# A decoder block with 32 experts on one core: order of the first value products, of the first experts' residues, and of six embedding products

## What is computed

```
h = rmsnorm(x, mix_norm);  proj = h @ w_in
ya = hgrn2_mix(...);  yb = retention_mix(...)
merged = sigmoid(ga) * (ya @ w_branch_a) + sigmoid(gb) * (yb @ w_branch_b)
x = x + merged @ w_out
h2 = rmsnorm(x, ffn_norm)
x = x + hier_moe(h2, ...)      # y_e = (silu(x_e @ w_gate) * (x_e @ w_up)) @ w_down, weighted sum of 2 experts
hp = rmsnorm(x, ple_norm)
x = x + sigmoid(hp @ w_ple_gate) * (p @ w_ple_proj)
return rmsnorm(x, final_norm)
```

## Time and profile before

| | us |
|---|---|
| timed executions | 1492.79, 1492.96, 1490.2 |
| median | 1492.79 |
| the profiled execution | 1489.6 |
| its span, first to last instruction | 1487.8 |
| PE busy | 1431.0 |
| DVE busy | 765.4 |
| ACT busy | 597.1 |
| GpSimd busy | 77.2 |

### The profile page before, as it was taken

One profiled execution on the slowest core, in us unless ns is written; L12 is line 12 of the kernel. 1 busy time (PEld: TensorE's weight loads), 2 busy tenths in 40 slices (PEclk: granted clock), 3 DMA queues, 4 the chain that ended last, 5 costly groups with the idle time before them and its releaser, 6 DMA issues.

```text
span 1487.8 us, 19084 instructions
## 1 busy us (share of the span) xinstructions
PE 1431.0 (96%) x7882; PEld 1192.9 (80%) x7882; DVE 765.4 (51%) x963; ACT 597.1 (40%) x731; POOL 77.2 (5%) x71
## 2 busy tenths in 40 slices
PE   6999999999999999999999999997899999998998
PEld 5888778877887888788888889986788888876886
DVE  5520266655553444221221125246799999987654
ACT  4410222212323322211111113243688888887555
POOL 0000000000000000000000000002122222211000
PEclk9999999999999999999999999998899999998999
DMA  6200111016220111221122218313899999995231
GB/s 242 85 2 0 49 30 30 15 32 154 57 57 8 50 54 39 67 68 56 60 63 63 63 50 299 133 71 129 348 372 384 391 381 393 384 369 214 85 107 64
DMA packets 103807, 205.26 MB, mean 138 GB/s; under 512 B 12976, under 2 KB 73008, under 8 KB 90160
## 3 DMA queue, kind: packets, MB, share of 16 engines
q1 hardware_dynamic: 93184, 182.89, 34.9%
q0 software_dynamic: 9248, 16.80, 3.0%
q10 hardware_dynamic: 1296, 4.46, 0.7%
HBM read 187.86 MB, written 28.84 MB: 146 GB/s over the span
## 4 chain that ended last, share of the span: by engine, by line
PE 52%; DVE 2%; DMA 1%; ACT 1%; issue 1%; POOLq 0%; DVEq 0%; ACTq 0%; SPq 0%
PE two_banks L176 8%; PE two_banks L178 8%; PE two_banks L177 8%; PE two_banks L2528 4%; PE two_banks L2529 4%; PE two_banks L2530 4%; PE two_banks L2411 2%; PE two_banks L2657 2%; PE two_banks L2413 2%; PE two_banks L2412 2%; PE two_banks L2658 2%; PE two_banks L2659 2%; PE two_banks L2518 2%; PE two_banks L2447 1%; DVE two_m_lo L1530 0%
## 5 line engine op out<-in xcount | busy, mean ns | idle before, releaser
L1332 DVE TENSOR_TENSOR two_chunk_lo<-two_chunk_raw,two_hi 128x2048 fp32r<-128x2048 f32 x96 | 217.2, 2286 | 21.8 <-ACT two_hi L1328 20.8
L1328 ACT CAST two_hi<-two_chunk_raw 128x2048 fp32r<-128x2048 f32 x96 | 180.9, 1917 | 7.3 <-DMA two_chunk_raw<-w_e 6.8
L223 DVE TENSOR_TENSOR mix_w_lo<-mix_w_raw,mix_w_hi 128x1024 fp32r<-128x1024 f32 (+1 forms) x51 | 58.5, 1148 | 194.0 <-ACT mix_w_hi L219 194.0
L176 PE MATMUL front_sums<-mix_hT_hi,mix_w_hi 128*128 128x512 f32 x320 | 127.7, 399 | 2.0 <-ACT reten_raw L892 2.0
L178 PE MATMUL front_sums<-mix_hT_hi,mix_w_lo 128*128 128x512 f32 x320 | 124.9, 390 | 0.0
L177 PE MATMUL front_sums<-mix_hT_lo,mix_w_hi 128*128 128x512 f32 x320 | 124.6, 389 | 0.0
L2528 PE MATMUL two_banks<-two_hi,two_xT_hi 128*128 128x512 f32 x256 | 104.0, 406 | 2.5 <-DVE two_xT_lo L1716 1.9
L219 ACT CAST mix_w_hi<-mix_w_raw 128x1024 fp32r<-128x1024 f32 (+1 forms) x51 | 50.4, 988 | 138.4 <-PE two_banks L178 88.2
L2530 PE MATMUL two_banks<-two_hi,two_xT_lo 128*128 128x512 f32 x256 | 101.5, 396 | 0.0
L2529 PE MATMUL two_banks<-two_chunk_lo,two_xT_hi 128*128 128x512 f32 x256 | 101.4, 396 | 0.0
L176 PE MATMUL two_banks<-mix_hT_hi,mix_w_hi 128*128 128x512 f32 x224 | 87.1, 389 | 0.0
(11 more groups left out here) (316 smaller groups left out, 3026.0 us busy)
## 6 DMA issues: line engine op xcount, KB each, us to landing
two_chunk_raw<-w_e SPq DMA_DIRECT2D x102, 1024.0 KB
mix_w_raw<-w_in SPq DMA_DIRECT2D x44, 512.0 KB, 3.9
two_r<-results SPq DMA_DIRECT2D x16, 512.0 KB, 4.9
vals_w_raw<-w_in SPq DMA_DIRECT2D x12, 512.0 KB, 8.2
heads_values<-x SPq DMA_DIRECT2D x8, 512.0 KB, 10.4
reten_swapped<-reten_raw SPq DMA_DIRECT2D x8, 512.0 KB, 6.3
mix_w_raw<-w_b SPq DMA_DIRECT2D x8, 512.0 KB, 4.6
two_x<-x SPq DMA_DIRECT2D x8, 512.0 KB, 7.4
```

What stands on the lines that cost most here:

```text
L176: nc.tensor.matmul(out, sh, mh, start=(k == 0), stop=False)
L223: self.nc.vector.tensor_tensor(self.lo[:, u, 0:kt], self.raw[:, u, 0:kt], self.hi[:, u, 0:kt].bitcast(F32), ALU.subtract).then_inc(self.lo ...
L1328: self.nc.scalar.copy(self.high(n)[:], self.raw(n)[:]).then_inc(self.hi_ok, 1)
L1332: self.nc.vector.tensor_tensor(self.low(n)[:], self.raw(n)[:], self.high(n)[:].bitcast(F32), ALU.subtract).then_inc(self.lo_ok, 1)
```

## The change

In the first stage PE transposes tile 0, does products(0, 0), then transposes tile 1; from there tile t + 1 is transposed in the middle of products(0, t). ACT and DVE take their steps in the order that goes with it: all four weight quarters first, then tile 1's scaling.

Around the first gathers, residue 0 moves ahead of the wait for the slot products, residue 1 behind the weight operations and ahead of first_x_lo, and in expert 0 both residues 2 and 3 go ahead of the product with silu. ACT makes the first four high parts in one go. owners and the read of its count move from behind residue 1 to the end of expert 1.

In the last stage LEAD is 4. ACT copies four products (the third and fourth to y, whose scatters must have ended), in the order 1, 0, 2, 3. Five products stand ahead of turn_rows(0), the sixth behind it, two are left in the loop. ACT splits all f first, and DVE's residues of f 4 and 5 move ahead of the first add_experts(0). The scatter of the last expert has a semaphore of its own.

```diff
-LEAD = 2
+LEAD = 4
...
             high(0)
-            weights(0, 1)
+            for n in range(1, QUARTERS):
+                weights(0, n)
             square(1)
             root(1)
-            weights(0, 2)
-            weights(0, 3)
-            high(1)
             for t in range(TT):
+                if t + 1 < TT:
+                    high(t + 1)
                 if t + 2 < TT:
                     square(t + 2)
                     root(t + 2)
-                    high(t + 2)
...
+            def products(b, t, halfway=None):
                 for k in range(KT):
+                    if k == 4 and halfway is not None:
+                        turn(halfway)
...
             turn(0)
+            products(0, 0)
             turn(1)
-            for t in range(TT):
-                products(0, t)
-                if t + 2 < TT:
-                    turn(t + 2)
+            for t in range(1, TT):
+                products(0, t, t + 1 if t + 1 < TT else None)
...
+            chunks.split_lo(dve, 0)
             dve.wait_ge(slots_mm, 1)
...
-            chunks.split_lo(dve, 0)
             weights()
+            chunks.split_lo(dve, 1)
             first_x_lo()
-            chunks.split_lo(dve, 1)
-            owners()
-            more_tiles = further_tiles(dve)
...
                 chunks.split_lo(dve, ahead[0])
+                if e == 0:
+                    chunks.split_lo(dve, ahead[1])
...
                     x_lo(e + 1)
-                    chunks.split_lo(dve, ahead[1])
+                    if e:
+                        chunks.split_lo(dve, ahead[1])
                     chunks.split_lo(dve, ahead[2])
+                if e == 1:
+                    owners()
+                    more_tiles = further_tiles(dve)
...
-                    for k in range(2):
-                        f_split(4, k)
                     dve.wait_ge(rows_in[0], 16)
...
+                if t >= 2:
+                    act.wait_ge(scattered[3 - t], 16 * len(range(3 - t, EXPERTS - 1, YS)))
+                A.copy(kept_product(t), banks_at(proj_bank(t), 2)).then_inc(proj_kept, 1)
...
-            f_split(3)
-            keep_product(0)
-            f_split(4)
-            keep_product(1)
-            f_split(5)
+            for n in range(3, FINALS):
+                f_split(n)
+            for t in (1, 0, 2, 3):
+                keep_product(t)
...
+                elif t >= LEAD:
+                    pe.wait_ge(proj_kept, t - 1)
...
-            for t in range(LEAD + 2):
+            for t in range(LEAD + 1):
                 proj(t)
             turn_rows(0)
+            proj(LEAD + 1)
```

More of the change, by code:

```diff
@@ L2162, in _ @@
             act.wait_ge(out_full, 16)
-            chunks.split_hi(act, 0)
-            chunks.split_hi(act, 1)
+            for n in range(HI_SLOTS):
+                chunks.split_hi(act, n)
             act.wait_ge(placed, marks["exps"])
@@ L2176, in _ @@
                     chunks.place_of(e, 2)]
-                chunks.split_hi(act, ahead[0])
+                if e:
+                    chunks.split_hi(act, ahead[0])
                 if e >= 2:
@@ L2187, in _ @@
                     x_hi(e + 1)
-                    chunks.split_hi(act, ahead[1])
+                    if e:
+                        chunks.split_hi(act, ahead[1])
                     chunks.split_hi(act, ahead[2])
```

41 lines of the change are left out of this document (21 added, 20 removed).

## The result

| | before | changed |
|---|---|---|
| timed executions, us | 1492.79, 1492.96, 1490.2, 1492.2 | 1482.18, 1480.86, 1479.95, 1478.08 |
| median | 1492.49 | 1480.4 |
| the profiled execution | 1489.6 | 1482.18 |
| its span | 1487.8 | 1480.3 |
| PE busy | 1431.0 | 1430.6 |

The ratio is 0.9923, 95% interval 0.9907 to 0.9939: 12.1 us less, and faster. The forecast was 1480.1 us. The two profiled executions are only 7.5 us apart, though. That the median came out as forecast doesn't show that each term did, so each is looked up.

A forecast was written before the change was run, and what follows sets the result against it. PE, always busy, was taken as the bound: only its idle or slow-clock time counts. Gains of 2.5 + 1.3 + 8.9 = 12.7 us, taken from the 1492.8 us median, gave 1480.1 us; range 1476 to 1485 us.

The forecast's parts named there:

- part B: Around the first gathers: residues moved, owners moved to expert 1's end; 1.3 us gained, bounds +2.0 and -0.9 us.
- the first one: Rival at the first gather: moving residue 0 doesn't release it, the middle gains 0, time 1481.4 us; chance 0.10.
- Part A: First stage: tile 0's products directly follow its transposes; 2.5 us gained, bounds 3.3 and 1.7 us, or 0.1 us.
- the gap: First stage, behind tile 1's transposes: PE newly idle for about 1.1 us before tile 1's products.
- rise at 16.4 us: First stage: the clock rises 5.2 us after continuous work begins, leaving 12 slow and 12 fast matmuls in tile 0's products.
- The wait for tile 2: First stage, middle of tile 1's products: tile 2's scaled rows ready at 24.1 us, wanted at 23.8; 0.2 us more.
- Rival two: First stage: the new 1.1 us idle time brings back the slow clock, leaving 0.1 us gained, 1482.5 us; chance 0.09.
- The terms for PE: First experts: the first gather ends sooner, 2.0 us gained; owners delays experts 2 and 3, 2.1 us lost.
- transfers issued up to 2 us sooner: Experts 0 and 1: earlier weight transfers set the experts' end, removing 0.6 to 2.0 us of PE's 2.0 us loss.
- Part C: Last stage: residues and products moved ahead of tile 0's transposes; 8.9 us gained, bounds 5.4 and 9.3 us.
- The 0.3 us ahead of the transposes and the 0.3 us between the halves: Last stage: PE waits 0.3 us after product five before tile 0's transposes, and 0.3 us more between their halves.
- the residues' move: Last stage: four residues go into VectorE's 6.45 us wait, ending PE's gap and slow gate products; 3.5 us.

The follow-up runs named there:

- A and C together: Kernel before with only the first stage's and the last stage's changes, all around the gathers as before: 1480.28 us, ratio 0.9917 to the kernel before.
- the copy: Kernel before with residue 0, beside the first gather, made by a plain one-input copy (results not the reference's): timed once, 1488.58 us.
- its repeat: The changed kernel run once more, unedited, on another chip: 1481.7 us, ratio 0.9929 to the kernel before.
- part B alone: Kernel before with only the change around the gathers (residues 0 and 1, expert 0's order, owners after expert 1): 1491.69 us, ratio 1.0008.
- part A alone: Kernel before with only the first stage's change: 1489.58 us, ratio 0.9992 to the kernel before.

## Why the forecast was right, and where it was not

**The sum.** 2.5 + 1.3 + 8.9 us had been forecast. The profiles give 1.9 to 2.2, about 0, and 8.9: 11 us. The medians gave 12.1 us on one chip and 9.4 us on another. The forecast of 12.7 us is above all three. That the median of the changed kernel came out within 0.3 us of 1480.1 us is in part luck: the 1.3 us of part B never came, and the profiles find only 11 us. None of the rivals took place as it was put, though the first one's value for part B came true for another reason.

**Part A** was forecast as 2.5 us, and the start of the products (11.2 forecast, 11.11 us found) and the gap (1.1 and 0.96 us) are right. The size is 2.2 us over all profiles; the 3.3 us of the first pair, the forecast's upper bound, belong to these two executions. What differs is when the clock rises. In the eight profiles with part A the spacing is down to 0.23 us at 14.1 to 16.7 us, mean 15.4, behind seven to twelve matmuls; in the six without it at 17.5 to 20.7 us, mean 19.1. The changed kernel's first profile is at the early end of the one (14.2 us) and the profile of before near the late end of the other (20.1 us). The forecast's rise at 16.4 us with twelve slow matmuls is what the profile of A and C together has (16.44 us). So the prediction took one execution's rise for the kernel's, and 29.90 us for a state that the six profiles reach at 29.4 us on average; with part A it is reached at 27.2 us (27.4 forecast). Why the moment varies the runs don't show. The wait for tile 2 (0.2 us) didn't come.
Rival two didn't take place: behind the gap, which is 0.96 us in all eight profiles with part A, the first matmul takes 0.50 us and the next 0.39 or 0.40 us.

**Part B** was forecast as 1.3 us and is worth nothing. The terms for PE are right: 2.1 us sooner at the first transposes from tok (7.45 us before, 5.34 us after; 2.0 forecast), and 2.1 us lost to owners (2.1 forecast, though the two gaps add up to only 1.55 us; the rest of the 2.1 us lies between them; the forecast's 1.36 and 0.72 us are also 0.06 and 0.05 us more than its own times give). From tok to the gather of expert 8 the profiles without a slow stretch near 1056 us have 46.4 to 46.6 us without part B (45.4 us with the copy) and 46.4 to 46.7 us with it. The step that failed is the next one: that transfers issued up to 2 us sooner set the end and would take 0.6 to 2.0 us off; for the 0.6 us the prediction gives no working either. I had read that the transfers were behind PE at 1280 us, and took them to have been so since expert 1. They fall behind only from expert 4 on, by 1 us an expert, and what happened to them earlier is forgotten. The time from issue to landing along the stage tells it in the profile of the changed kernel; that of before has none of these landings on record.

**Part C** was forecast as 8.9 us, and each profile shows it: 1487.8 - 1354.36 = 133.44 us and 1480.3 - 1355.75 = 124.55 us in the first pair. The 0.3 us ahead of the transposes and the 0.3 us between the halves leave no gap in the rows, and no slow clock followed. How it was split was off: the residues' move is worth 4.1 us, not 3.5, and 4.8 us are left for the products. They cover one another, so the share of one depends on which is taken away first.

**The profiled pair** differs by 4.7 us less than its parts, and the experiments explain it as two executions at opposite ends. Tok was written at 1036.17 us in the profile of before, the earliest of the six without part A. From tok to the last stage the changed one took 320.8 us, the longest of fourteen. One more slow stretch ahead of tok is in it (two against one), shown here for the changed kernel, with PEclk, the mean clock of a window, in the third column from the end:

```profile
478.00:484.00 6.00, 6.00 (x24) 5.08 (x25) 3.61 (x4) 2.69 (x4) 0.00 (x0) 0.72 0.66 179
1006.00:1012.00 6.00, 6.00 (x26) 4.95 (x26) 4.24 (x12) 0.00 (x0) 0.00 (x0) 0.72 0.09 33
```

0.28 x 6 us make 1.7 us of full clock for each (3.4 us at half), and its lead over before falls by 1.4 and 1.1 us there. Ahead of the first of the two windows PE had stood idle:

```profile
477.91 1.60 PE L1240 MATMUL gate_turned<-kept_ident,gate_scaled 128*128 128x128 f32 x8 [2.21 <-DVE gate_scaled L1187]
```

Why the transfers were slower in that execution from 1100 to 1140 us (landings of 12.7 us, where its repeat had 11.5 and part B alone 9.6) stays open.

## What to carry to other kernels

Before a head start of a transfer is counted, look at the time from issue to landing along the stage: behind its lowest point (8 us here) the transfers fell back, a head start from before that point was forgotten, and what PE had won by then reached the end. A helper step of DVE is free only in a place where the engine's own idle time is longer than the step, and the timeline of the engine gives that place (3.59 us ahead of expert 0's product here, for 2.7 us of owners). When parts of a change are worth 1 to 2 us each and executions vary by as much, measure the distance between two marks of one profile, over several profiles, and not the whole time. And take the moment at which the clock rises from several profiles: the same start gave 14.1 to 16.7 us here.

## What the runs showed of the hardware

- A gather instruction on GpSimd waits for the end of a VectorE pass that reads only SBUF and runs when it is issued, also of one with a single input: 1.91 us beside a copy of 1.23 us, 2.98 us beside a subtraction of 2.29 us, 0.99 us alone. Two half passes let it through after the first. A pass with an input from PE's banks, with 0.57 us left, did not hold it (0.99 us).
- Stretches of 3.4 us at the lower clock level come up at five places, near 212, 332, 480, 1008 and 1057 us, in some executions and not in others of the same code; two executions of the changed kernel had three and one. At four of the places PE had just stood idle, for 2.34, 2.02, 2.21 and 1.87 us, and the clock fell between 0.3 us before and 1.5 us after the end of that. The same idle times (1.7 to 1.9 us at the last place) stand in all fourteen profiles, with the fall or without it, so they alone don't decide it. Near 1008 us PE had no gap of 0.2 us or more in the 12 us before the fall. One stretch costs 1.0 us near 1008 us, 1.4 us near 480 us, and 1.5 us near 1057 us (10.60 and 9.12 us between the gathers of experts 5 and 6 in the kernel before and in part A alone).
- The clock's first rise in the kernel comes at a different time in each execution: 3.0 to 5.3 us after the first product with part A, 1.0 to 4.4 us after it without.
